# A two-block sequence model on one core: the mixed branch's norm by token with rows, the roots' column by transfers, the last rows weighted by ScalarE

## What is computed

```python
def _layernorm(x, w, b, eps=LN_EPS):
    mu = jnp.mean(xf, axis=-1, keepdims=True)
    var = jnp.mean(jnp.square(xf - mu), axis=-1, keepdims=True)
    y = (xf - mu) * lax.rsqrt(var + eps)
    return (y * w + b)

def _spatial_gating_branch(u_raw, v_raw, g_raw, ln_w, ln_b, w_s, b_s):
    u = jax.nn.gelu(u_raw)
    v = _layernorm(jax.nn.gelu(v_raw), ln_w, ln_b)
    vc = v.reshape(b, s // SG_CHUNK, SG_CHUNK, SG_GROUPS, SG_GROUP_CH)
    mixed = jnp.einsum('gts,bnsgc->bntgc', w_s, vc) + b_s.T[None, None, :, :, None]
    return u * mixed.reshape(b, s, SG_WIDTH) * jax.nn.silu(g_raw)

# second_block: h = rmsnorm(x); h @ w_in is split into q, two gates, i, ga, u, v, gb, ma, mb
    merged = (jax.nn.sigmoid(ma_raw) * jnp.einsum('bsw,wd->bsd', y_a, w_proj_a)
              + jax.nn.sigmoid(mb_raw) * jnp.einsum('bsw,wd->bsd', y_b, w_proj_b))
    x = x + jnp.einsum('bsd,de->bse', merged, w_out)
    return _rmsnorm(x, final_norm_w)
```

## Time and profile before

| | |
|---|---|
| median of 3 runs | 1702.16 us (1702.12 to 1702.25) |
| the profiled execution | 1701.79 us, of which the span of the profile is 1700.0 us |
| TensorE, matmul | 1688.2 us busy, 99% of the span |
| TensorE, weight load | 1392.8 us, 82% |
| VectorE | 1141.7 us, 67% |
| ScalarE | 814.1 us, 48% |
| GpSimd | 30.7 us, 2% |
| granted clock of TensorE | 0.998 of full speed |
| DMA | 174.82 MB, mean 103 GB/s |

### The profile page before, as it was taken

One profiled execution on the slowest core, in us unless ns is written; L12 is line 12 of the kernel. 1 busy time (PEld: TensorE's weight loads), 2 busy tenths in 40 slices (PEclk: granted clock), 3 DMA queues, 4 the chain that ended last, 5 costly groups with the idle time before them and its releaser, 6 DMA issues.

```text
span 1700.0 us, 22047 instructions
## 1 busy us (share of the span) xinstructions
PE 1688.2 (99%) x8742; PEld 1392.8 (82%) x8742; DVE 1141.7 (67%) x1687; ACT 814.1 (48%) x1167; POOL 30.7 (2%) x57
## 2 busy tenths in 40 slices
PE   9999999999999999999999999999999999999998
PEld 7888888878887888888888888888888888888886
DVE  7754346878886645677776344667888777878574
ACT  6223234765756323322222334666667577665522
POOL 0000000000000000000000000100000000000000
PEclk9999999999999999999999999999999999999999
DMA  5234232333332222332233333542222222222332
GB/s 208 96 99 127 99 100 89 122 100 104 120 105 82 96 92 98 99 99 91 95 100 99 103 107 112 202 145 77 86 78 84 75 87 75 88 86 76 118 105 87
DMA packets 50550, 174.82 MB, mean 103 GB/s; under 512 B 5872, under 2 KB 8048, under 8 KB 50320
## 3 DMA queue, kind: packets, MB, share of 16 engines
q1 hardware_dynamic: 45200, 155.45, 27.7%
q0 software_dynamic: 5248, 17.96, 3.3%
HBM read 164.93 MB, written 4.26 MB: 100 GB/s over the span
## 4 chain that ended last, share of the span: by engine, by line
PE 98%; DMA 1%; DVE 1%; ACT 0%; issue 0%; SPq 0%; DVEq 0%; ACTq 0%
PE bank L582 83%; PE bank L688 4%; PE bank L602 2%; PE bank L882 2%; PE bank L798 1%; PE bank L894 1%; PE bank L796 1%; PE bank L756 1%; DMA raw<-stream 0%; PE bank L908 0%; PE bank L667 0%; PE bank L920 0%; PE bank L777 0%; DVE X L2250 0%; PE bank L922 0%; PE bank L924 0%
## 5 line engine op out<-in xcount | busy, mean ns | idle before, releaser
L582 PE MATMUL bank<-u_high,w_high 128*128 128x512 f32 x1504 | 592.1, 394 | 0.0
L582 PE MATMUL bank<-u_high,w_low 128*128 128x512 f32 x1504 | 585.8, 389 | 0.0
L582 PE MATMUL bank<-u_low,w_high 128*128 128x512 f32 x1504 | 585.1, 389 | 0.0
L993 ACT ACTIVATE w_high<-raw 128x1024 fp32r<-128x1024 f32 x283 | 298.9, 1057 | 573.5 <-PE bank L582 559.8
L1567 DVE TENSOR_TENSOR w_low<-raw,w_high 128x1024 fp32r<-128x1024 f32 x282 | 344.7, 1223 | 253.5 <-ACT w_high L993 247.8
L582 PEld LDWEIGHTS bank<-u_high,w_high 128*128 128x128 f32 x1504 | 282.4, 188 | 59.6 <-issue 2.7
L582 PEld LDWEIGHTS bank<-u_high,w_low 128*128 128x128 f32 x1504 | 282.3, 188 | 59.6
L582 PEld LDWEIGHTS bank<-u_low,w_high 128*128 128x128 f32 x1504 | 282.6, 188 | 57.9 <-issue 1.0
L1658 DVE TENSOR_TENSOR h_raw<-bank,rs 128x512 f32<-128x512 f32 x44 | 30.4, 691 | 61.8 <-PE bank L582 55.0
L582 PE MATMUL bank<-f_high,w_high 128*128 128x512 f32 x176 | 68.5, 389 | 0.0
L582 PE MATMUL bank<-f_low,w_high 128*128 128x512 f32 x176 | 68.5, 389 | 0.0
(11 more groups left out here) (393 smaller groups left out, 2497.3 us busy)
## 6 DMA issues: line engine op xcount, KB each, us to landing
raw<-stream SPq DMA_DIRECT2D x283, 512.0 KB, 3.3
rows<-running POOLq DMA_DIRECT2D x32, 256.0 KB, 3.5
X<-x_t SPq DMA_DIRECT2D x8, 256.0 KB, 4.8
residual<-X POOLq DMA_DIRECT2D x4, 512.0 KB, 4.7
u_high<-n_high_rows POOLq DMA_DIRECT2D x4, 512.0 KB, 8.4
u_low<-n_low_rows POOLq DMA_DIRECT2D x4, 512.0 KB, 9.5
X<-residual POOLq DMA_DIRECT2D x4, 512.0 KB, 5.4
masks_f<-masks SPq DMA_DIRECT2D x1, 1280.0 KB, 6.0
```

The lines of the kernel that those rows point to most:

```text
L582: ins = pe.matmul(acc[:], w[:, k], x[:, at + k], start=start and k == first and j == 0, stop=stop and k == KT - 1 and j == 2)
L993: act.activation(w_high[:, n % HI_RING], raw[:, n % RAW_RING], ACT.Copy).then_inc(hi_done, 1)
```

## The change

- `roots_by_token` is gone. GpSimd, when `rs_b` is ready, writes one partition's row of it to memory (`roots`), waits, and reads it back as a column of four values per partition into `r_tok`. ScalarE waits for that before it evicts the first v batch. These two transfers stand ahead of `ws_t` on GpSimd's queue.
- `token_sums` and `biases` are gone. The weight and bias of the norm lie in memory as two rows (`ln_rows`), and one transfer of 1 MB copies them to all partitions, into the upper half of `Ya`, whose space the spilled rows have left: it waits for all four spills, and stands ahead of the four pairs on GpSimd's queue.
- `normed(c)` is two operations with a wait between them, (v + mean) * w and that times scale plus b, each with a tensor of 128 x 1024 as second source. It has moved from the prologue to head 0, steps 3, 4, 6 and 9.
- The finish of a mixed row is an add.
- In the last blocks ScalarE multiplies each finished row 0 to 6 by its final weight, behind its square. VectorE then multiplies the rows of a half by the root in groups of 2, 3 and 2 rows, and row 7 alone with its weight; the second half's `last_row` stands behind the first group. Each half is written in transfers of 2, 3 and 3 rows.

```diff
@@ -191,7 +191,7 @@
-    out = [("roots",)]
+    out = []
@@ -217,6 +217,9 @@
+FINAL_ROWS = [(0, 2), (2, 3), (5, 2), (7, 1)]
+FINAL_TRANSFERS = [(0, 2, 1), (2, 3, 2), (5, 3, 4)]
@@ -554,12 +560,12 @@
-            for half, rows in enumerate((4, 2)):
+            for half in range(2):
                 ts_ = slice(half * T // 2, half * T // 2 + T // 2)
-                for k in range(0, KT, rows):
-                    sp.wait_ge(s_fin, half * KT + k + rows)
+                for k, rows, done in FINAL_TRANSFERS:
+                    sp.wait_ge(s_fin, half * len(FINAL_ROWS) + done)
...
@@ -859,10 +850,6 @@
-                if key == ("vt", 0, 2):
-                    roots_by_token()
-                if key == ("b", 0):
-                    token_sums()
@@ -1313,17 +1300,15 @@
-                if key == ("vt", 0, 2):
-                    act.wait_ge(t_done, TURN[("roots",)] + 1)
-                    act.activation(r_tok, side[2][:, 0:NCH], ACT.Copy).then_inc(t_free, 1)
-                    act.wait_ge(t_free, TURN[("roots",)] + 1)
+                if key == ("vt", 0, PER_BATCH - 1):
+                    act.wait_ge(s_roots, 32)
@@ -1539,7 +1524,9 @@
                 if j:
+
                     square(3, j - 1, X2[:, j - 1])
+                    act.activation(X2[:, j - 1], X2[:, j - 1], ACT.Identity, scale=pcol("final_norm_w_2", j - 1)).then_inc(x_weighted, 1)
@@ -1966,18 +1953,13 @@
             def normed(c):
+
+                dve.wait_ge(m_done, 1)
                 dve.wait_ge(v_dev, 1)
+                dve.wait_ge(s_ln, 16)
                 x = VG[:, :, c * P:(c + 1) * P]
-                ts(x, x, v_mean[:, c:c + 1], v_scale[:, c:c + 1], ALU.add, ALU.mult).then_inc(v_normed, 1)
...
+                link(stt(x, x, v_mean[:, c:c + 1], ln_w, ALU.add, ALU.mult))
+                stt(x, x, v_scale[:, c:c + 1], ln_b, ALU.mult, ALU.add).then_inc(v_normed, 1)
@@ -1993,12 +1975,6 @@
-                if key == ("b", 0):
-                    normed(0)
-                    normed(1)
-                if key == ("q", 0):
-                    normed(2)
-                    normed(3)
@@ -2110,7 +2086,6 @@
                     diff(0, 1)
-                    biases()
@@ -2150,6 +2125,8 @@
+                if h == 0 and q in (3, 4, 6, 9):
+                    normed((3, 4, 6, 9).index(q))
@@ -2246,10 +2225,15 @@
+                dve.wait_ge(x_weighted, KT - 1)
+                for k, rows in FINAL_ROWS:
+                    if half == 0 and k == 2:
                         last_row(1, side[2])
+                    if k < KT - 1:
+                        x = X2[:, k:k + rows, ts_]
+                        tt(x, x, rs[:, ts_].rearrange("p (o t) -> p o t", o=1).to_broadcast([P, rows, T // 2]), ALU.mult).then_inc(s_fin, 1)
...
@@ -2269,13 +2253,19 @@
-            wait_block(pool, ("vt", 0, 0))
+
+            pool.wait_ge(r_done, 1)
+            pool.dma_start(roots, rs_b[0:1, :]).then_inc(s_roots, 16)
+            pool.wait_ge(s_roots, 16)
+            pool.dma_start(r_tok, bass.AP(roots.tensor, roots.offset, [[1, P], [P, NCH]]), allow_slow_non_contiguous=True).then_inc(s_roots, 16)
             pool.dma_start(ws_t[:], ws_in).then_inc(s_ws, 16)
...
             pool.dma_start(bs_row[:], bass.AP(bs_in.tensor, bs_in.offset, [[0, P], [P, KT], [1, P]])).then_inc(s_bs, 16)
+            pool.wait_ge(s_spill, 16 * KT // 2)
+            pool.dma_start(Ya[:, 4:8].rearrange("p a t -> p (a t)"), bass.AP(ln_in.tensor, ln_in.offset, [[0, P], [1, 2 * D]])).then_inc(s_ln, 16)
```

51 lines of the change are left out of this document (19 added, 32 removed).

## The result

| kernel | median us | lowest to highest | runs | ratio to before, 95% interval |
|---|---|---|---|---|
| before | 1702.20 | 1701.35 to 1702.75 | 20 | |
| changed | 1704.99 | 1701.94 to 1706.50 | 20 | 1.0015 [1.0009, 1.0021] |

The changed kernel is 0.15% slower. That is inside the 0.2% that the prediction takes for what a measurement can tell, but the forecast was 1699.5, which is faster, and the time lies outside of its range. The second column to look at is the spread: 4.6 us where the kernel before has 1.4. The profiled execution of the changed kernel took 1703.98 us with a span of 1702.1; before it was 1701.79 and 1700.0.

The account below looks back on a forecast made before the run. TensorE, busy in 99% of the span, was taken to bound the kernel. The terms -0.90 - 1.71 - 0.34 + 0 + 1.2 - 0.9 = -2.65 us, from the median of 1702.16, gave 1699.5; range 1698.0 to 1702.4.

Parts of the forecast that it names:

- What bounds the kernel: TensorE, busy 99% of the span: only its own stream, its waits and the tail behind its last matmul move the end.
- Part 1: Roots' column by transfers instead of TensorE's matmuls: -0.90 us, the gather hidden if r_tok comes until 1060.6.
- Rival (c): Slow gather of r_tok in 4-byte pieces: past 1064 the gain is gone, at 15 us the end is 1709; chance 0.07.
- Part 2: Token sums removed (-1.71 us) and stall behind them (-0.34); load of Tb, end of ("b", 0), takes 4.6 us.
- the stall: TensorE's wait at q's bank, 0.80 us where 0.46 is ordinary: 0.34 us, to be gained in full.
- a line in order of issue: Loads queue behind what was issued earlier; five transfers ahead explained the 8.4 us of the load of Tb.
- turn-taking: Skill's rule that DMA engines alternate between queues, read as landing within about twice 1.3 us; set aside for the 8.4 row.
- Rival (b): Load of Tb still takes 8.4 us, 1.8 us return as a wait: 1701.3 to 1702.3; chance 0.18.
- Part 3: Backlog moved back onto the load issued at q's end, landing about 1110.6, cast needed by 1111.0: 0, at worst +1.0 us.
- Part 4: Norm moved into head 0, its step 9 operations delaying the pair TensorE needs: +1.2 us, bounds 0 to 1.6.
- Rival (a): Head 0 swallows the norm, so its cost there is 0: -3.85 us, 1698.3; chance 0.17.
- Part 5: Last rows, VectorE's grouped operations and the output transfers: -0.9 us, bounds -0.4 and -1.1.

Follow-up runs that it names:

- e7: Kernel before with only the roots' column changed, fetched by two GpSimd transfers instead of TensorE's small matmuls and ScalarE's copy: 1701.45 us, ratio 0.9995.
- e6: Kernel before with only the change's last-rows part (ScalarE weights rows, VectorE multiplies grouped rows, three transfers a half): 1701.18 us, ratio 0.9993.
- e3: Changed kernel with u transfers, then rows, issued only after the load issued at the end of ("b", 0) has landed: 1699.80 us, ratio 0.9984.
- e9: Kernel before without the two token-sum matmuls and the eight bias-building instructions, the norm's bias term left out of the result: 1702.05 us, ratio 0.9999.
- e15: Changed kernel with the rows issued on the end of ("b", 0), behind the load instead of 0.05 us ahead: 1704.18 us, ratio 1.0010.
- e13: Changed kernel with u transfers and rows held until the load landed, and the norm's fourth chunk in step 8 of head 0: 1698.49 us, ratio 0.9978.
- e11: Changed kernel with the rows last and the first six u transfers released by the same event as the load: 1700.16 us, ratio 0.9988.
- e10: Changed kernel with the rows left beside the load and the eight u transfers held until that load has landed: 1702.01 us, ratio 1.0001.
- e2: Changed kernel with the norm's fourth chunk moved from step 9 to step 8 of head 0: 1703.87 us, ratio 1.0008.
- e8: Changed kernel with 14 unread matmuls added for TensorE just before its wait for q's bank: 1703.02 us, ratio 1.0005.
- e4: Changed kernel with ScalarE's eviction of q's bank placed ahead of the cast of the late load: 1703.28 us, ratio 1.0005.
- e14: Changed kernel with the rows laid out 128 times in DRAM, a source of its own for each partition: 1704.50 us, ratio 1.0010.
- e12: Changed kernel with the rows' 1 MB in two transfers of 512 KB, pieces of 4 KB instead of 8 KB: 1703.44 us, ratio 1.0003.
- e1: Changed kernel with the rows' 1 MB transfer issued behind the eight u transfers instead of before them: 1701.63 us, ratio 1.0000.

## Why the prediction was wrong, step by step

- **What bounds the kernel.** Right: TensorE has no slack up to q's bank or behind it, and e7, e6 and e3 each moved the end by what they moved in its stream, in its waits or in the tail.
- **Part 1, -0.90.** Right. e7 measured 0.90. The gather of 4-byte pieces took 4.5 us where decay_b's took 4.4, and no engine waited for it. Rival (c) fell with it. Its 15 us was also no "twice the longest of any transfer here": u_low's transfers took 10.6 us in the kernel before. The two DMA issues of the changed kernel (KB, us to landing):

```profile
roots<-rs_b POOLq DMA_DIRECT2D x1, 2.0 KB, 1.6
by_token<-roots POOLq DMA_DIRECT2D x1, 2.0 KB, 4.5
```

- **Part 2, -2.05: the step that failed.** Its first half, that the load does not move with the sums and that a slow load takes them back, is what e9 showed: -0.30, with 8.0 us for the load. Its second half failed: "ahead of the load of Tb only bs_row is left ... 4.6 us". In its place: the load took 9.4 us, TensorE stood for 3.3 us, and the whole 2.05 came back. The rows' transfer was issued at 1095.62, the load at 1095.67, so the rows were there with it, and three pairs of u rows followed at once. The order of the two is not what went wrong: the prediction's own numbers put the rows 0.1 us behind the load (1096.8 - 0.9 for Tb at 1096.7 - 0.9), and e15, which does put them behind, measured the same 9.4. What failed is that transfers with or behind the load cost it nothing. With only the rest of bs_row beside it the load takes 3.9 to 4.3 us (e3, e13), a little less than the 4.6 of the working; the change doesn't leave it that alone. The 0.34 of the stall is small beside what the load varies by: e6 and e7, with 8.1 and 8.3 us for the load where the kernel before has 8.4, show no such step at all.
- **The picture under it, a line in order of issue,** fell too. What is issued behind a load costs it as well (e11: 2.7 us), and so does what is issued beside it (e10: 4.7 us). The 8.4 of the earlier trace rows had been read as speaking against turn-taking, because five transfers lay ahead of that load; two more were issued 0.3 and 0.8 us behind it, and the row can't tell the two apart. The Trainium skill (DMA: Bandwidth & Descriptors, Queues, rings and completion order) says that an engine takes turns between its queues one packet at a time and drains a whole packet before it turns. By that, transfers behind a load may cost it, as e11 shows. It doesn't give the 4.7 us of e10, nor does the prediction's "within about twice its own 1.3 us" follow from it: that took the engines to run at the full rate and all 16 alike, and beside the load they did neither.
- **Rival (b)** (chance 0.18, "the 1 MB lands on it") named what happened and priced it at 1701.3 to 1702.3. It was 1.0 us too cheap for the load (9.4 for 8.4), and had nothing for the clock.
- **The clock, +1.66,** stood in no part and no rival. It is what turned "nothing gained" into "slower" (the four executions at a clock of 0.999 have a median of 1702.57), and it makes the runs spread. In the profiled executions where TensorE's step at this place was 1.9 us or less, the 84 matmuls took 19.4 us; in all six with 2.49 us or more they took 20.7 to 21.0.
- **Part 3, 0.** Right: the load issued at q's end landed 7.3 us later, at 1108.4, earlier than the 1110.6 worked out and than the 1111.0 allowed.
- **Part 4, +1.2.** Right in place and near in size: 1.16 us of waiting behind the pair, 1.4 with the spacing beside it; VectorE's wide operations took 1.28 each for the 1.22 of the working; e2 and e13 got back 1.1 and 1.3. Rival (a) fell.
- **Part 5, -0.9.** Right, at its far bound of 1.1: 1.17 in e6, 1.1 in the profile.
- **The sum.** With Part 2 true it would have stood: e3, which moves GpSimd's transfers and nothing else, measured 1699.80 for the 1699.5 forecast.

## What to carry to other kernels

A term that removes work from an engine is worth nothing while a transfer that ends later bounds the same place; before it goes into the sum, ask of that transfer what else is in the DMA engines from its issue to its landing, issued before, with or after it, and not only what is ahead. A pause of TensorE is to be priced with what its clock does behind it, and if a pause can't be avoided, matmuls that nobody reads may be cheaper than idling (e8: 2.0 us). Bulk transfers that nobody needs for 30 us, as the rows here, can wait for the landing of the load that somebody does need; here that was worth 5 us (e3).

## What the runs showed of the hardware

- A load of 512 KB took 3.9 us with only the rest of an earlier transfer beside it (e3), 6.6 with six transfers of 512 KB issued from 0.27 us behind it on (e11), 8.6 with one of 1 MB issued at the same time (e10), and 9.4 to 10.2 with both that and u transfers behind it (changed kernel, e2, e4, e8, e14, e15). Pieces of 8 KB from a shared source or from one for each partition, issued 0.05 us before or 0.3 us after the load, made no difference; with pieces of 4 KB it was 8.6 us (e12). The reason is open.
- The engines moved 153 to 261 GB/s from 1099 to 1102 us with load, rows and u transfers under way, where they move 408 to 422 at other times. They moved 389 with the rows alone but for two late signals of the load (e10), and 154 for 2 us without the rows (e11).
- In one and the same load nine of the 16 completion signals came after 3.3 us and seven after 8.1 to 9.4 (changed kernel).
- TensorE's clock fell to its lower level at each of the six steps of 2.49 to 3.80 us at q's bank, for 3.4 us each time, and that cost 1.4 to 1.7 us. It fell between 0.5 us before TensorE came back (e14) and 1.5 us after (e2). In the profiled executions it didn't fall behind steps of 0.86 and 1.90 us there, nor behind one of 2.9 us at 1123 to 1126 (e4); slower executions of e1 and e4, with a mean clock 0.001 or 0.002 lower, may differ. So the length of the stand is not all of it; what else counts is open.
- The two-step gather through DRAM (2 KB out, 1.6 us; 512 pieces of 4 bytes back, 4.5 us) took about as long for its second half as a transfer of 64 KB on the same queue (4.4 us).
